# Strassen's seven products for 16 of 22 pairs of feed-forward up-projection tiles, on one Trainium2 core

## What is computed

```python
def conv_ffn(u, w_up, conv_w, conv_b, w_down):
    hdn = causal_dwconv(u @ w_up, conv_w) + conv_b
    gate, val = jnp.split(hdn, 2, axis=-1)
    return (jax.nn.silu(gate) * val) @ w_down
...
        u = rms_norm(x, norm_gains[layer, 2])
        ff = conv_ffn(u, ffn_w_up[layer], ffn_conv_w[layer], ffn_conv_b[layer], ffn_w_down[layer])
        x = x + rms_norm(ff, norm_gains[layer, 3])
```

## Time and profile before

| | |
|---|---|
| median of 3 runs | 1746.18 us (1744.74 to 1747.45) |
| span of the profiled execution | 1745.5 us; the profile gives no other time of it, so the span stands for it |
| granted clock of TensorE, mean | 0.997 of 2.4 GHz |
| busy: TensorE | 1699.3 us, 97% |
| busy: VectorE, ScalarE, GpSimd | 1082.7, 851.6, 443.2 us |
| layer 0's tiles 4 to 43 on TensorE | about 390.6 to 608.2 us of the span |

### The profile page before, as it was taken

The page is one execution under the profiler, slowest core; times in us unless marked ns, Lnnn a source line. Parts: engine busy times, 40 slices in busy tenths (PEclk is TensorE's granted clock), DMA queues, the critical chain, the costliest instruction groups (busy, mean ns, idle before and its releaser), DMA issues. The chain is left out here.

```text
span 1745.5 us, 23896 instructions
## 1 busy us (share of the span) xinstructions
PE 1699.3 (97%) x8362; PEld 1385.4 (79%) x8362; DVE 1082.7 (62%) x1684; ACT 851.6 (49%) x1459; POOL 443.2 (25%) x341
## 2 busy tenths in 40 slices
PE   9999999999999999999999999999999999999997
PEld 6787887778888878778888887888888876777785
DVE  6637444387666643588788858766663367888353
ACT  6757545354333332466556645433342244455573
POOL 1445444101111110035554630111111003232232
PEclk9999999999999999999999999999999999999999
DMA  5311111222222222311211212222222222121121
GB/s 220 135 41 73 37 38 67 74 89 97 96 96 96 96 97 96 108 51 59 73 62 60 73 49 99 83 96 96 96 96 97 96 97 100 48 86 60 49 73 48
DMA packets 40373, 144.25 MB, mean 83 GB/s; under 512 B 4563, under 2 KB 4819, under 8 KB 39781
## 3 DMA queue, kind: packets, MB, share of 16 engines
q1 hardware_dynamic: 40292, 143.20, 23.2%
HBM read 141.05 MB, written 2.13 MB: 82 GB/s over the span
## 5 line engine op out<-in xcount | busy, mean ns | idle before, releaser
L190 PE MATMUL bank<-u_high,w_high 128*128 128x512 f32 x1556 | 635.8, 409 | 7.8 <-DVE w_low L582 2.0
L192 PE MATMUL bank<-u_high,w_low 128*128 128x512 f32 x1556 | 609.1, 391 | 0.0
L191 PE MATMUL bank<-u_low,w_high 128*128 128x512 f32 x1556 | 607.6, 390 | 0.0
L190 PEld LDWEIGHTS bank<-u_high,w_high 128*128 128x128 f32 x1556 | 293.3, 188 | 79.5 <-issue 19.7
L192 PEld LDWEIGHTS bank<-u_high,w_low 128*128 128x128 f32 x1556 | 292.6, 188 | 63.3
L191 PEld LDWEIGHTS bank<-u_low,w_high 128*128 128x128 f32 x1556 | 293.6, 189 | 58.0 <-issue 4.1
L154 ACT ACTIVATE w_high<-w_ring 128x1024 fp32r<-128x1024 f32 x228 | 239.2, 1053 | 185.1 <-PE bank L192 160.2
L163 DVE TENSOR_TENSOR w_low<-w_ring,w_high 128x1024 fp32r<-128x1024 f32 x175 | 220.2, 1263 | 159.6 <-ACT w_high L154 159.1
L163 POOL TENSOR_TENSOR w_low<-w_ring,w_high 128x1024 fp32r<-128x1024 f32 x53 | 127.5, 2415 | 336.6 <-ACT w_high L154 336.6
L928 ACT ACTIVATE conv_up<-bank,col_sb 128x512 f32<-128x512 f32 x88 | 68.6, 779 | 263.5 <-DVE bank L988 263.5
L1057 POOL TENSOR_TENSOR hidden<-conv_up 128x512 f32 x44 | 58.2, 1323 | 488.0 <-DVE conv_up L999 364.1
(11 more groups left out here) (427 smaller groups left out, 2363.3 us busy)
## 6 DMA issues: line engine op xcount, KB each, us to landing
w_ring<-ffn_up SPq DMA_DIRECT2D x88, 512.0 KB, 3.5
w_ring<-ffn_down SPq DMA_DIRECT2D x44, 512.0 KB, 3.4
w_ring<-c_in SPq DMA_DIRECT2D x32, 512.0 KB, 3.5
w_ring<-g_in SPq DMA_DIRECT2D x16, 512.0 KB, 3.5
w_ring<-m_in SPq DMA_DIRECT2D x12, 512.0 KB, 7.8
w_ring<-fox_in SPq DMA_DIRECT2D x12, 512.0 KB, 4.3
w_ring<-dsa_in SPq DMA_DIRECT2D x12, 512.0 KB, 3.4
w_ring<-ab_out SPq DMA_DIRECT2D x8, 512.0 KB, 4.1
```

Source lines behind the costliest of these rows:

```text
L190: nc.tensor.matmul(out, a[0], b[0], start=start, stop=False)
L191: nc.tensor.matmul(out, a[0], b[1], start=False, stop=False)
L192: return nc.tensor.matmul(out, a[1], b[0], start=False, stop=stop)
```

## The change

The last 16 of the 22 pairs of each layer are computed by a variant of Strassen's scheme. A pair is a 2x2 block problem: two rows of outputs (gate tile, value tile), two halves of the input channels (4 blocks of 128 each), two halves of the tokens (256 each). In place of eight products of half size it has seven, called a11, s1, a22, s2, s4, a12, s3 after their weight operand. a11, a12 and a22 are 128x512 pieces of the weight tiles; s1 to s4 are sums and differences of pieces, made on GpSimd (`add`). Each of the seven pieces is split, highs on ScalarE, lows on VectorE but for that of a22, which GpSimd makes. Their token operands are halves of the tokens or sums of them (`tokens`), made once a layer; for these, the tokens are normalised before (GpSimd: eight multiplications by `rn`, four sums of 1024 columns; ScalarE and VectorE: seven splits of 1024 columns), so that the 32 changed tiles have no take. Each product is 12 matmuls of 256 columns. Intermediate results are copied out of their bank on ScalarE (`keep`, three of 256 columns) and added back on VectorE (`combine`, three of 256 columns). Tiles 4 to 11 of `ffn` stay as they were. The pairs' weights go through six buffers (`w_more` is the third pair's), and everything in the phase is now written out, with no hardware loop in the up projection. Weights need about the same DMA bytes as before.

```diff
+HALF = T // 2
+SEQUENCE = ("a11", "s1", "a22", "s2", "s4", "a12", "s3")
+PLACE = {"a22": 0, "s4": 1, "a12": 2, "s3": 3, "a11": 4, "s1": 5, "s2": 6}
+SUMS = ("s1", "s2", "s4", "s3")
...
+def nth(i, name, pairs):
+
+    n = SEQUENCE.index(name)
+    if name == "a22":
+        return 7 * pairs if i == pairs - 1 else 7 * (i + 1) + n
+    return 7 * i + n if i else (n + 1 if n < 2 else n)
+
...
+    def high(self, act, i, name):
+        k = self.k
+        if name in SUMS:
+            act.wait_ge(self.summed, self.sum_at(i, name))
+        else:
+            self.loaded(act, i, 1 if name == "a22" else 0)
+        if i:
+            self.wait_multiplied(act, i - 1, name)
+        k.nc.scalar.activation(self.place(name, 0), self.piece(i, name), ACT.Copy).then_inc(self.high_done, 1)
...
+    def low(self, eng, i, name):
+        eng.wait_ge(self.high_done, nth(i, name, self.pairs))
+        ins = eng.tensor_tensor(self.place(name, 1), self.piece(i, name), self.place(name, 0).bitcast(F32), ALU.subtract)
+        ins.then_inc(self.last_low if name == "a22" else self.low_done, 1)
...
+    def add(self, pool, i, name):
+        k, a = self.k, lambda row, half: self.raw(i, row)[:, half * T:half * T + T]
+        if name == "s1":
+            self.loaded(pool, i, 0)
+            self.loaded(pool, i, 1)
+        elif name != "s3":
+            pool.wait_ge(self.summed, self.sum_at(i, name) - 1)
+        if i:
+            pool.wait_ge(self.low_done, self.low_at(i - 1, name))
+        x, y, op = {
+            "s1": (a(1, 0), a(1, 1), ALU.add),
+            "s2": (self.sums[:, 0, :], a(0, 0), ALU.subtract),
+            "s4": (a(0, 1), self.sums[:, 1, :], ALU.subtract),
+            "s3": (a(0, 0), a(1, 0), ALU.subtract)}[name]
+        k.nc.gpsimd.tensor_tensor(self.sums[:, SUMS.index(name), :], x, y, op).then_inc(self.summed, 1)
...
+    def product(self, pe, i, name, free):
+        k = self.k
+        if name == "a22":
+            pe.wait_ge(self.last_low, i + 1)
+        else:
+            pe.wait_ge(self.low_done, self.low_at(i, name))
+        kind = {"s1": "z", "s4": "z", "a12": "y"}.get(name, "x")
+        start = name in ("a11", "s1", "a12")
+        if start:
+            free(i, kind)
+        elif name == "s2":
+            self.wait_kept(pe, i, 0)
+        elif name == "s4":
+            self.wait_kept(pe, i, 1)
+        elif name == "s3":
+            self.wait_kept(pe, i, 2)
+        else:
+            self.wait_combined(pe, i, 2)
+        out, moving = self.bank(i, kind)[:, 0:HALF], self.tokens[name]
+        for m in range(4):
+            w = [self.place(name, n)[:, m * P:m * P + P] for n in range(2)]
+            k.nc.tensor.matmul(out, w[0], moving[0][:, m, :], start=start and m == 0, stop=False, skip_group_check=not start)
+            k.nc.tensor.matmul(out, w[0], moving[1][:, m, :], start=False, stop=False, skip_group_check=not start)
+            ins = k.nc.tensor.matmul(out, w[1], moving[0][:, m, :], start=False, stop=m == 3, skip_group_check=not start)
+        ins.then_inc(self.multiplied, 1)
...
+    def keep(self, act, i, which):
+
+        k = self.k
+        self.wait_multiplied(act, i, ("a11", "s1", "s2")[which])
+        if i > 1:
+            self.wait_combined(act, i - 2, (1, 2, 0)[which])
+        bank = self.bank(i, "z" if which == 1 else "x")
+        k.nc.scalar.activation(self.held(i, which), bank[:, 0:HALF], ACT.Copy).then_inc(self.kept, 1)
...
+    def combine(self, dve, i, which, free=None):
+
+        k, nc = self.k, self.k.nc
+        x, y, z = (self.bank(i, s) for s in "xyz")
+        if which == 0:
+            self.wait_kept(dve, i, 2)
+            self.wait_multiplied(dve, i, "a12")
+            out, bank, kept = y[:, HALF:T], z[:, 0:HALF], self.held(i, 2)
+        elif which == 1:
+            self.wait_multiplied(dve, i, "a12")
+            out, bank, kept = y[:, 0:HALF], y[:, 0:HALF], self.held(i, 0)
+        else:
+            self.wait_multiplied(dve, i, "s3")
+            out, bank, kept = x[:, HALF:T], x[:, 0:HALF], self.held(i, 1)
+        nc.vector.tensor_tensor(out, bank, kept, ALU.add).then_inc(self.combined, 1)
...
+            for i in range(PAIRS):
+                product(i, "a11")
+                product(i, "s1")
+                if i:
+                    product(i - 1, "a22")
+                for name in ("s2", "s4", "a12", "s3"):
+                    product(i, name)
...
+                nxt = i < PAIRS - 1
+                sv.keep(act, i, 0)
+                if nxt:
+                    sv.high(act, i + 1, "a11")
+                silu(gate(i - 1) // 2)
+                sv.keep(act, i, 1)
+                if nxt:
+                    sv.high(act, i + 1, "s1")
+                else:
+                    sv.wait_multiplied(act, i, "s1")
+                    k.go(second)
+                    k.split_high(act, 2, 0)
+                    kt.src(act, 0)
+                tap(val(i - 1))
+                sv.high(act, i, "a22")
+                sv.keep(act, i, 2)
+                if nxt:
+                    sv.high(act, i + 1, "s2")
+                    sv.high(act, i + 1, "s4")
+                    sv.high(act, i + 1, "a12")
+                else:
+                    k.split_high(act, 3, 0)
+                    kt.src(act, 1)
+                tap(gate(i))
+                if nxt:
+                    sv.high(act, i + 1, "s3")
+            silu(gate(PAIRS - 1) // 2)
+            tap(val(PAIRS - 1))
 ...
+            low(6)
+            low(7)
             dve.wait_ge(opened.rooted, 1)
-            step(0)
-            step(1)
-            with dve.Fori(2, n - 1) as i:
-                ch.loop(4, i - 2)
-                step(i)
-            ch.end(n - 3)
-            step(n - 1)
-            k.go(second)
-            k.split_low(dve, 3, 1)
-            kt.rest(dve, 1)
+            take(0)
+            take(1)
+            conv(0)
+            take(2)
+            conv(1)
+            low(8)
+            take(3)
+            conv(2)
+            take(4)
+            conv(3)
+            low(9)
+            take(5)
+            conv(4)
+            token("s1")
+            take(6)
+            conv(5)
+            low(10)
+            take(7)
+            conv(6)
+            low(11)
+            take(8)
+            conv(7)
+            token("s3")
+            token("s2")
+            take(9)
+            conv(8)
+            conv(9)
+            sv.low(dve, 0, "a11")
+            sv.low(dve, 0, "s1")
+            take(10)
+            token("a11")
+            token("a22")
+            take(11)
+            sv.low(dve, 0, "s2")
+            sv.low(dve, 0, "s4")
+            token("s4")
+            token("a12")
+            sv.low(dve, 0, "a12")
+            conv(10)
+            sv.low(dve, 0, "s3")
+                nxt = i < PAIRS - 1
+                if nxt:
+                    sv.low(dve, i + 1, "a11")
+                    sv.low(dve, i + 1, "s1")
+                else:
+                    k.go(second)
+                    k.split_low(dve, 2, 0)
+                    kt.rest(dve, 0)
+                conv(val(i - 1))
+                if nxt:
+                    sv.low(dve, i + 1, "s2")
+                if nxt:
+                    sv.low(dve, i + 1, "s4")
+                else:
+                    k.split_low(dve, 3, 1)
+                sv.combine(dve, i, 0)
+                sv.combine(dve, i, 1)
+                if nxt:
+                    sv.low(dve, i + 1, "a12")
+                else:
+                    kt.rest(dve, 1)
+                sv.combine(dve, i, 2)
+                conv(gate(i))
+                if nxt:
+                    sv.low(dve, i + 1, "s3")
+            conv(val(PAIRS - 1))
...
+            for m in range(4):
+                normalise(m)
+            mul(0)
+            token("s1")
+            for m in range(4, 6):
+                normalise(m)
+            mul(1)
+            for m in range(6, KD):
+                normalise(m)
+            token("s3")
+            mul(2)
+            token("s2")
+            token("a22")
+            sv.add(pool, 0, "s1")
+            sv.add(pool, 0, "s2")
+            mul(3)
+            sv.add(pool, 0, "s4")
+            sv.add(pool, 0, "s3")
+            sv.add(pool, 1, "s1")
+            mul(4)
+            for i in range(PAIRS):
+                if i < PAIRS - 1:
+                    for name in ("s2", "s4", "s3"):
+                        sv.add(pool, i + 1, name)
+                sv.low(pool, i, "a22")
+                mul(gate(i - 1) // 2)
+                if i < PAIRS - 2:
+                    sv.add(pool, i + 2, "s1")
+            mul(gate(PAIRS - 1) // 2)
```

More of the change, by code:

```diff
@@ L471, in product @@
         k = self.k
[L472 removed]
+        ins = k.product(k.ps[m][:, :], [x[:, m * P:(m + 1) * P] for x in k.ws[2 + s]], [x for x in self.sp2[s]], start, stop)
         if stop:
@@ L848, in _, with pair, released @@
             k.go(first)
[L849 to L852, removed]
+            def pair(i):
```

(47 more changed lines are left out.)

234 lines of the change are left out of this document (203 added, 31 removed).

## The result

The kernel after takes 1762.23 us (median of 4 runs, 1761.93 to 1764.17); beside it the kernel before took 1746.09. The ratio is 1.0093, 95% interval 1.008 to 1.0105: 0.93% slower, 16 us. The forecast was 1757.6 us in a range of 1734 to 1782, slower with a chance of 0.66; the added time is 16 us where 11.4 were forecast.

What follows compares the result with a forecast made beforehand. TensorE bounds the kernel before; afterwards VectorE and GpSimd taking turns would set the rounds. Per layer 18.3 + 15 x 10.67 + 1.44 = 179.8 us against 174.1, two layers +11.4, giving 1757.6 us, range 1734 to 1782.

Steps and rivals of the forecast that it cites:

- TensorE's step: Changed pairs: 256-column matmuls start 0.12 us apart, so a pair takes 10.08 us on TensorE instead of 10.88.
- the clock: TensorE's granted clock, at the 2.4 GHz level in the kernel before, was taken as no term.
- The turns at the port: Two-SBUF-operand operations of VectorE and GpSimd run one at a time, a turn costing 0.55 us on VectorE, 1.15 on GpSimd.
- The bound from port time: Per pair, six GpSimd operations and six VectorE lows need at least 10.2 us of port time, above TensorE's 10.08.
- the placing: One round's VectorE and GpSimd operations placed in order by hand: 10.67 us a round, bounds 10.08 and 11.3.
- The run-up: Stretch before and through pair 0's six products: they end at 452.5 instead of 442.8, 9.7 us lost, bounds 2 and 15.
- The sum for a layer: Pair 0's products, 15 rounds and the last a22: 179.8 us against 174.1, +5.7 us a layer.
- The end: Passage from the last pair to the down projection: priced at zero, at most 2 us a layer.
- TensorE as the bound at 10.08: Rival for the rounds: port turns meet less often, giving 1740 us, or 1725 with a short run-up; chance 0.24.
- GpSimd winning nearly each turn: Rival for the rounds: VectorE waits 0.9 us at each low, rounds of 11.5 to 12, 1783 to 1795 us; chance 0.07.
- Instruction supply: Rival: the 256-column stream cannot hold 0.12 us; 0.13 a matmul gives 10.9 us a pair, 1764 or more; chance 0.03.

Runs made afterwards that it cites:

- e2_no_sums: The kernel after without GpSimd's four sums of weight blocks, s1 to s4 being plain pieces, so part of the computation is missing: 1733.81 us.
- e6_a22_sum_first: The kernel after with the low of a22 on VectorE and, on GpSimd, sum s1 ahead of the multiplication: 1764.92 us.
- e8_two_moved: The kernel after with the low of a22 and sum s3 moved from GpSimd to VectorE, GpSimd's other sums ahead of its multiplication: 1747.6 us.
- e3_a22_on_vector: The kernel after with the low of a22 moved from GpSimd to VectorE, behind conv(val): 1795.63 us.
- e1_silu_later: The kernel after with ScalarE's silu of pair 5 moved behind keep(0, 1) in the first round: 1763.13 us.
- e5_two_moved_silu: e8_two_moved with, in addition, ScalarE's silu of pair 5 moved behind keep(0, 1): 1741.53 us.
- e9_token_a22_last: e5_two_moved_silu with the token split of a22 moved from before the last take to behind low s3 of pair 0: 1740.49 us.

## Why the prediction was right, and where it was off

**TensorE's step.** Of the 2687 steps between the new matmuls of the kernel after some 2570 are 0.11 to 0.13 us; TensorE alone gives 10.08 (e2_no_sums), as forecast. What the forecast put at nothing was the clock: in the run-up of layer 0, 27 steps of 0.213 fell at the 1.2 GHz level (last section). After the hole at s4 they make 1.1 of the 1.4 us by which pair 0's six products ended later than forecast (453.9 for 452.5).

**The turns at the port.** Shown, as far as turns go: the mechanism was the forecast's, and e2_no_sums, e6_a22_sum_first and e8_two_moved bear it out from three sides. No run shows that it is a port which the two engines share; what the runs show is the turns and their price. The round was placed at 10.67 and is 10.82, where a low behind GpSimd ends 0.55 us after it and GpSimd's 1.15 after a low, nearly as read from the earlier trace rows. In the round above I had low s3 waiting and sum s3 behind it; both are there, with s3 starting at 566.78. Before, a pair took 10.88, so the steady state gives back almost nothing: 0.06 us a pair.

**The bound from port time.** "At least 10.2" was only a bound and was not the cause. e3_a22_on_vector lowered it and was slower by 33 us. The prediction used the placing for its number, which took the order in; the expectation of e3_a22_on_vector used the sum and failed.

**The run-up.** The starts were forecast well: a11 at 436.0 (measured 436.10), low s3 at 447.7 (it ran from 446.95 to 447.64), s4 at 448.2 (448.12). What failed is what the term stands for: "9.7 us lost" was booked as a loss of TensorE's, with the silu as its last cause. e1_silu_later took the silu's part away and gained nothing. The loss was on the path because VectorE was late, and TensorE's hole only overlapped it.

**The sum for a layer.** +5.7 forecast. From the first matmul of the opening in front to the start of the last high-by-high matmul of the down projection, layer 0 takes 371.06 us (366.61 to 737.67) against 363.31 (366.39 to 729.70), and layer 1 371.04 (1068.38 to 1439.42) against 363.21: +7.8 each, +15.6 together; the rest of the program took 1.0 us less in this execution. The missing 2.1 us a layer come above all from the join between run-up and rounds; the 15 rounds themselves are 160.9 us for 160.1. I joined the rounds to the end of pair 0's six products on TensorE (452.5, measured 453.9), where VectorE's combine in front of a22 (measured 455.3) sets them. From there, 13 rounds of 10.83, then 10.39 and 9.81 give 616.2 for the last combine. The last a22 starts at 616.78 and ends 1.44 later; less the 1.36 us of the two bank groups already done, that is 616.9, where the kernel before stood at 608.2. Of these 8.7 us, 0.2 is the later opening, and 0.7 is regained in the down projection, which waits less in its own first steps than before; 7.8 are left. The end was priced at zero, and TensorE waits there about 1.0 us for that combine.

**The rivals.** TensorE as the bound at 10.08, with the silu's hole still in, is what e8_two_moved reaches, at 1747.6; 1740 was reckoned for it, 7.6 too little. e5_two_moved_silu comes near that number, with 1741.5, but with a shorter run-up, so the agreement is chance. GpSimd winning nearly each turn, put at rounds of 11.5 to 12, is near e3_a22_on_vector's case, rounds of 11.8. Instruction supply played no part: e2_no_sums holds 0.12 us a matmul through its rounds.

## What to carry to other kernels

In this kernel VectorE's operations with two SBUF operands and GpSimd's elementwise ones take turns (1.15 us for GpSimd's 128x512, 0.55 for VectorE's). So price them as one queue, and then place them in order: a GpSimd operation is free only under a VectorE operation that reads PSUM, and what GpSimd waits for decides whether it is there at that time. Before a hole in the bounding engine's timeline is counted as a loss, ask which engine sets the next meeting point; taking the 6 us hole of each layer away gave nothing, and 6 us for both layers together once the rounds were TensorE's. A scheme that saves 12.5% of the columns with matmuls half as wide saved 7.4% of TensorE's time for a pair (10.08 for 10.88 us), and that only where the other engines kept up.

## What the runs showed of the hardware that was not expected

After TensorE stood for 6 us, its matmuls of 256 columns started 0.213 us apart instead of 0.12: 12 steps in a row from 448.47 to 451.03 in layer 0, and 19 from 1150.21 in layer 1. That is 256 columns at the 1.2 GHz level, and the granted clock of the stretch is 0.50:

```profile
448.20:451.10 2.90, 2.90 (x14) 2.90 (x15) 2.58 (x4) 2.27 (x5) 2.49 (x2) 0.50 0.00 0
```

Another 15 such steps came from 437.70 to 440.90, after a stand of only 1.84 us that had ended at 436.10. Each such stretch costs 1.1 to 1.8 us on top of the hole. A stand does not always bring it: in e5_two_moved_silu one of 2.47 us in front of s3 of pair 0 was followed by 15 slow steps in layer 0 and by none at the same place in layer 1, and in e9_token_a22_last one of 2.46 us, ended at 449.86, by none. What decides is open.
